# VectorE turns the next job's rows behind its readings of the gate and up banks instead of ahead of both

## The reference, cut to what matters

```python
xb = xt[tok]
gate = jnp.minimum(xb @ w_gate[e] + b_gate[e], SWIGLU_LIMIT)
up = jnp.clip(xb @ w_up[e] + b_up[e], -SWIGLU_LIMIT, SWIGLU_LIMIT)
act = (up + 1.0) * gate * jax.nn.sigmoid(SWIGLU_ALPHA * gate)
return act @ w_down[e] + b_down[e]
```

## Time and profile before

| | |
|---|---|
| median of 3 runs | 2375.02 us (2374.65 to 2375.45) |
| the profiled execution | 2374.8 us, of which its span is 2373.1 us |
| TensorE, matmuls | 2184.6 us busy, 92% of the span |
| VectorE | 1006.6 us busy, 42% |
| ScalarE, GpSimd | 452.7 us, 445.9 us, 19% each |
| TensorE in 590 to 2300 us | 1636.2 us busy of 1710.0 |

### The profile page before, as it was taken

One profiled execution on the slowest core, in us unless ns is written; L12 is line 12 of the kernel. 1 busy time (PEld: TensorE's weight loads), 2 busy tenths in 40 slices (PEclk: granted clock), 3 DMA queues, 4 the chain that ended last, 5 costly groups with the idle time before them and its releaser, 6 DMA issues.

```text
span 2373.1 us, 32923 instructions
## 1 busy us (share of the span) xinstructions
PE 2184.6 (92%) x9893; PEld 1013.8 (43%) x9894; DVE 1006.6 (42%) x1548; ACT 452.7 (19%) x579; POOL 445.9 (19%) x418
## 2 busy tenths in 40 slices
PE   6889999779956999999999999999999999999992
PEld 2444444464543444443443344444444444444441
DVE  3675743556663143344424243423253333223234
ACT  2334443331110111111111111111111111101113
POOL 0010000001212123222222132312123222122110
PEclk9989999889968999999999999999999999999996
DMA  9221320012242576889479999747899558886634
GB/s 330 80 81 53 110 59 27 1 72 91 103 181 93 202 293 213 298 308 376 163 267 400 362 349 405 262 157 245 300 381 351 183 177 294 301 311 234 232 88 170
DMA packets 169077, 510.48 MB, mean 215 GB/s; under 512 B 16333, under 2 KB 51329, under 8 KB 167883
## 3 DMA queue, kind: packets, MB, share of 16 engines
q1 hardware_dynamic: 153914, 474.25, 53.4%
q0 software_dynamic: 15120, 35.67, 6.9%
HBM read 480.51 MB, written 31.46 MB: 216 GB/s over the span
## 4 chain that ended last, share of the span: by engine, by line
PE 85%; DVE 7%; DMA 4%; issue 2%; ACT 1%; SPq 1%; POOL 0%; another core or an unknown queue 0%; DVEq 0%; POOLq 0%; ACTq 0%
PE psall L585 27%; PE psall L613 14%; PE psall L589 10%; PE psall L756 10%; PE psall L594 5%; PE psall L617 5%; PE psall L744 3%; PE psall L867 2%; PE psall L861 2%; PE psall L622 2%; DMA arena<-in_w_down_dram 1%; PE psall L654 1%; PE psall L723 1%; DMA arena<-in_x_dram 1%; DVE arena L1352 1%
## 5 line engine op out<-in xcount | busy, mean ns | idle before, releaser
L585 PE MATMUL psall<-arena 128*128 128x512 f32 x1472 | 648.8, 599 | 20.9 <-DVE arena L1637 12.8
L585 PEld LDWEIGHTS psall<-arena 128*128 128x128 f32 x1472 | 279.9, 192 | 368.9 <-issue 355.9
L613 PE MATMUL psall<-arena 128*128 128x512 f32 x736 | 323.6, 598 | 5.6 <-DVE arena L1686 2.7
L589 PE MATMUL psall<-arena 128*64 128x512 f32 x1152 | 259.3, 602 | 9.5 <-DMA arena<-in_w_up_dram 4.4
L1637 DVE STREAM_TRANSPOSE arena<-arena 128x1024 f32<-128x1024 f32 x49 | 61.0, 1245 | 479.0 <-PE psall L585 307.4
L756 PE MATMUL psall<-arena 128*128 128x512 f32 (+1 forms) x608 | 246.5, 563 | 0.7 <-ACT arena L976 0.7
L613 PEld LDWEIGHTS psall<-arena 128*128 128x128 f32 x736 | 139.6, 191 | 184.2 <-issue 184.2
L1149 ACT COPY arena<-psall 128x512 f32<-128x512 f32 x49 | 28.7, 586 | 793.6 <-PE psall L654 793.6
L1686 DVE COPY arena<-psall 128x512 f32<-128x512 f32 x49 | 33.9, 691 | 321.7 <-PE psall L654 321.6
L756 PEld LDWEIGHTS psall<-arena 128*128 128x128 f32 x608 | 116.5, 192 | 120.6 <-issue 116.3
L1626 DVE TENSOR_TENSOR arena<-psall,arena 32x256 f32<-32x256 f32 (+2 forms) x123 | 79.9, 649 | 203.2 <-PE psall L613 154.3
(11 more groups left out here) (286 smaller groups left out, 2013.0 us busy)
## 6 DMA issues: line engine op xcount, KB each, us to landing
arena<-in_w_gate_dram SPq DMA_DIRECT2D x128, 1024.0 KB
arena<-in_w_up_dram SPq DMA_DIRECT2D x128, 1024.0 KB
arena<-in_w_down_dram SPq DMA_DIRECT2D x128, 1024.0 KB
arena<-in_w_ada_dram SPq DMA_DIRECT2D x16, 1024.0 KB, 5.3
arena<-in_w_ada_dram SPq DMA_DIRECT2D x4, 2048.0 KB, 14.3
arena<-in_w_in_dram SPq DMA_DIRECT2D x16, 512.0 KB, 4.1
arena<-in_x_dram SPq DMA_DIRECT2D x2, 2048.0 KB, 28.4
arena<-in_w_out_dram SPq DMA_DIRECT2D x1, 4096.0 KB, 13.8
```

What stands on the lines that cost most here:

```text
L585: mm = pe.matmul(ps[2 * g + s], xT[:, k, :], w[:, s * BANK:(s + 1) * BANK], start=(k == 0), stop=(k == KD - 1))
L589: mm = pe.matmul(ps[2 * g][HT * j:HT * j + HT, :], xT[:, k, HT:P], w[:, j * BANK:(j + 1) * BANK], start=(k == 0), stop=(k == KD - 1), skip ...
L613: mm = pe.matmul(ps[6 + s], aT[:, k, :], w[:, s * BANK:(s + 1) * BANK], start=(k == 0), stop=(k == KD - 1))
```

## The change

`swiglu` is cut in two. Its first half, the readings of the gate and up banks, keeps the name and now stands ahead of the turning of the next job's rows; the second half, the clip and the two products, becomes `gated_rows` and stands behind the turning, with a branch by kind of its own.

```diff
             def swiglu(u, kind):
                 parts, lo, hi = JOB_KINDS[kind]
-                s7 = 1.0 / (1.0 + math.exp(-SWIGLU * LIMIT))
                 dve.wait_ge(gu_used, u * GUP + GUP)
                 dve.wait_ge(bias_spread, order_)
...
                 mm.then_inc(gu_free, 1)
+
+            def gated_rows(u, kind):
+                parts, lo, hi = JOB_KINDS[kind]
+                s7 = 1.0 / (1.0 + math.exp(-SWIGLU * LIMIT))
                 w = slice(lo, hi)
                 dve.wait_ge(gu_free, u + 2)
...
                         job_row(dve, [typ_n, ord_n], u + 2)
+                        order_ = ord_of(dve, ord_c, wait_c)
+                        by_kind(dve, typ_of(dve, typ_c), lambda kind: swiglu(u, kind))
                         with dve.If(typ_of(dve, typ_n) > 0):
...
                             turn_rows_in()
-                        order_ = ord_of(dve, ord_c, wait_c)
-                        by_kind(dve, typ_of(dve, typ_c), lambda kind: swiglu(u, kind))
+                        by_kind(dve, typ_of(dve, typ_c), lambda kind: gated_rows(u, kind))
```

## The result

The changed kernel takes 2382.12 us (median of 20 runs, 2378.57 to 2389.47); the kernel before takes 2375.80 beside it (20 runs, 2373.45 to 2382.76). The ratio is 1.0023, with a 95% interval of 1.0014 to 1.0032: slower by 5.4 us, 3.3 to 7.6. The prediction was 2376.7 us, and no measurable change. The profiled execution after has a span of 2380.5 us, 7.4 above that of before.

The account below looks back on a forecast made before the run. TensorE, its matmuls busy 92% of the span, was taken as the bound. Term one added 1.7 us, terms two and three nothing: 2376.5 us on the profiled execution, 2376.7 from the median, range 2373.5 to 2381.

Parts of the forecast that it names:

- Term one: TensorE's start at nine jobs where VectorE's third step ends last: six 0.12 us later, three 0.32, together 1.7 us.
- The three long waits: TensorE's job starts behind kind 3 or at the first job, 3.7, 3.46 and 3.5 us; forecast barely longer.
- the two values weighed there: Idle behind kind 3's last reading: nothing by the skill's branch times (sum 0.6 us), or the trace's 0.36, which was taken.
- The first rival: The seam closes as VectorE's queue runs ahead over branches; nine places shift 0.1 us at most, 2375 us; chance 0.32.
- Term two: GpSimd's gather and what queues behind it: 2.36 us later behind full jobs, 6.5 behind kind 3; costed at nothing.
- SyncE behind kind 3: The later spread would end at 1282.1, 2.1 us before SyncE reaches its next bias row; no cost.
- The weighing's 0.26 us: Slack left before TensorE wants the copy, in a quarter job behind a full one; costed at nothing, up to 1 us possible.
- The 2.62 us: Slack before the change from the copy's end, 1855.36, to TensorE's need at 1857.98; less 2.36 it left 0.26.
- SyncE at rows 8's shape: First weights issued right after the spread behind a full job, four places, 2.36 us later, needed 18.3 us after issue; nothing.
- the price of the late gather: Term two's cost of GpSimd's gather, counter and spread coming later, set at nothing.
- The third rival: Late weights: spread 2.36 us later at four places reaches TensorE, 9.4 us, 2386 us; chance 0.11 including a late copy.
- Term three: Gate reading ends 1.3 us earlier, ScalarE's sigmoid too: no gain; the last job's clip nothing, at most 0.36 us.

Follow-up runs that it names:

- e15: The kernel before, with three more gather instructions per turn of GpSimd's loop, between spread and scatter, into an unread spare region: 2396.53 us, ratio 1.0077.
- e8: The kernel before, with GpSimd's spread of the gate and up bias moved behind the scatter: 2401.74 us, ratio 1.0100.

## Why the prediction was wrong, by its own steps

- Term one, the seams: too high. The turning begins 0.03 us behind a kind 3 job's up reading, not 0.36, and 0.09 ahead of the end of a full one (1852.78 against 1851.65 + 1.22). The three long waits are 10.6 us (7.0 in two, and 3.5) against 10.7 (3.7 and twice 3.5), and the short one is 0.22 as before: nothing instead of 1.7 us. Of the two values weighed there, the Trainium skill's (Advanced Engine Details and Errata, Control Flow Timing: 51 and 108 ns, so that the branching fits beside the running reading) agrees with the trace, and the nearest row, the idle of 0.36 us behind a quarter's product, didn't carry over. The first rival was right on this term.
- Term two, the gather later by 2.36 us: right within 0.2 (behind the full job of the earlier trace rows it begins 5.08 us behind the start of the down product, 1855.48 less 1850.40; before 2.89, 1845.65 less 1842.76). SyncE behind kind 3 not late: right. The weighing's 0.26 us: wrong, TensorE stood 0.38 us for the copy there. The 2.62 us that I took for slack were measured to a TensorE that the stretched product at 1846.64 had held up by 3.1 us. SyncE at rows 8's shape: nothing at that place, but late weights cost 1.4 and 2.1 us at two others.
- The step that failed is the price of the late gather in term two, which I set at nothing. I asked who waits for the gather and followed those chains. I didn't ask what the gather runs beside once it is later: narrow products, and e15 shows that this costs time. In the traces 4.8 of the 8.4 us stand there. The other 3.5 are late weights, a chain that I did follow and called free by a margin.
- The sign stood in the earlier trace rows. The L594 product that begins at 1846.64 beside four gather instructions is cut off at 29 of 64 multiplications. The kernel before goes on:
```profile
1849.88 0.39 PE L594 MATMUL psall<-arena 128*32 128x256 f32 x1 [0.33 <-issue]
1850.61 0.38 PE L594 MATMUL psall<-arena 128*32 128x256 f32 x1 [0.34 <-issue]
1851.33 2.10 PE L594 MATMUL psall<-arena 128*32 128x256 f32 x33 [0.35 <-issue]
```
  One multiplication in 0.7 us, where 64 take 3.66. I read that row for its start alone.
- The third rival, late weights: its mechanism is real (e8), but at 2.4 us it is, by the traces, the smaller part: 3.5 us at two places instead of 9.4 at four. The time it gave, 2386, was nearer, for the most part for another reason.
- Term three, the early reading: nothing, as predicted; no wait on ScalarE appeared.

## What to carry to other kernels

When a change makes a step later, list not only who waits for it but what it will run beside, transfers started by GpSimd above all. A row of many small instructions that the timeline cuts in pieces with "issue" between them is a cost already being paid: find what runs beside each cut before moving anything. And a wait that the profile names (here, the down weights) isn't the whole cause until a run that removes it gives the time back.

## What the runs showed of the hardware

TensorE's narrow products are held up by gather instructions beside them, by up to 3.9 us each (e15, near 1537). The queues need not be full: beside the product near 1145 in the changed kernel the transfers are at a share of 0.42 (1144 to 1146) and 0.26 (1146 to 1148). Long products (128x512) beside the same gathers keep their time: in the 17 traces 287 full down products had two or more gather instructions beside them, and all took 13.90 to 14.00 us.

The Trainium skill, Runtime: NRT & Kernel Launch, section Instruction fetch mechanics, says that an engine's instructions come in blocks of 16 KiB, 256 instructions, by a transfer of its sequencer's own, and that a taken branch out of the blocks at hand stalls. As an estimate from that page, the 64 multiplications and 64 weight loads of a narrow product use half a block in 3.66 us, more per microsecond than any other product here, which would fit that only the narrow ones suffer. The page of the changed kernel has such transfers:
```profile
q8 instruction: 26, 0.43, 0.1%
```
They are 16 KB each, but the last is at 765 us, in the first of the 49 jobs. What TensorE's fetch meets inside the loop no run here shows.
